# 64 bytes of padding ahead of the two large areas of a transformer kernel's SBUF

## The reference

```
x = x + 0.5 * swiglu(rms_norm(x))                       # ffn1: 1024 -> 2816 -> 1024
x = x + w_out @ (gated gMLP mixer + gated differential attention)   # mixer
x = x + 0.5 * swiglu(rms_norm(x))                       # ffn2
x = x + g1 * w_out_2 @ [S5 state space, sliding-window attention]   # mix2, modulated by c
x = x + g2 * conv_ffn(modulated rms_norm(x))            # ffn3: 1024 -> 2 x 2816, width-3 conv -> 1024
```

## Time and profile before

| what | value |
|---|---|
| time, median of 3 runs | 1828.91 us (1828.8 to 1830.04) |
| the profiled execution's own time | 1823.55 us |
| its span, first to last instruction | 1820.9 us |
| mean granted TensorE clock | 0.994 |
| TensorE busy | 1785.5 us |
| VectorE / ScalarE / GpSimd busy | 1057.2 / 727.5 / 184.5 us |

### The profile page before, as it was taken

One profiled execution on the slowest core, in us unless ns is written; L12 is line 12 of the kernel. 1 busy time (PEld: TensorE's weight loads), 2 busy tenths in 40 slices (PEclk: granted clock), 3 DMA queues, 4 the chain that ended last, 5 costly groups with the idle time before them and its releaser, 6 DMA issues. The chain is left out here.

```text
span 1820.9 us, 23599 instructions
## 1 busy us (share of the span) xinstructions
PE 1785.5 (98%) x8872; PEld 1454.9 (80%) x8872; DVE 1057.2 (58%) x1479; ACT 727.5 (40%) x1011; POOL 184.5 (10%) x239
## 2 busy tenths in 40 slices
PE   8999999999999999999899999999998999999998
PEld 6888888878888777888787888887986778888887
DVE  6666536564564666554789743436585556655433
ACT  3222222333444887423232322224556345555322
POOL 4222001210000000005211020120000400000000
PEclk9999999999999999999899999999999999999999
DMA  7767422333222212223555452335122223222222
GB/s 224 238 216 220 145 72 85 106 117 112 93 77 86 70 48 70 70 93 107 180 165 166 134 168 81 96 101 185 42 100 70 70 93 107 100 92 81 92 89 86
DMA packets 171692, 206.79 MB, mean 114 GB/s; under 512 B 18404, under 2 KB 150114, under 8 KB 171106
## 3 DMA queue, kind: packets, MB, share of 16 engines
q1 hardware_dynamic: 144994, 161.97, 27.5%
q0 software_dynamic: 12640, 38.55, 6.7%
q10 hardware_dynamic: 13984, 5.27, 1.1%
HBM read 190.29 MB, written 17.56 MB: 114 GB/s over the span
## 5 line engine op out<-in xcount | busy, mean ns | idle before, releaser
L662 ACT CAST w_hi<-w_raw 128x2048 fp32r<-128x2048 f32 x158 | 301.3, 1908 | 739.1 <-PE bank L1921 379.9
L1147 DVE TENSOR_TENSOR w_lo<-w_raw,w_hi 128x2048 fp32r<-128x2048 f32 x158 | 367.1, 2324 | 376.3 <-ACT w_hi L662 375.8
L1921 PE MATMUL bank<-h_hi,w_hi 128*128 128x512 f32 x1056 | 414.7, 393 | 6.5 <-DVE w_lo L1147 5.2
L1921 PE MATMUL bank<-h_hi,w_lo 128*128 128x512 f32 x1056 | 412.1, 390 | 0.0
L1921 PE MATMUL bank<-h_lo,w_hi 128*128 128x512 f32 x1056 | 326.3, 390 | 1.6 <-DVE h_lo L1185 1.6
L1921 PEld LDWEIGHTS bank<-h_hi,w_hi 128*128 128x128 f32 x1056 | 199.1, 189 | 51.3 <-issue 5.0
L1921 PEld LDWEIGHTS bank<-h_lo,w_hi 128*128 128x128 f32 x1056 | 198.7, 188 | 43.8 <-DVE h_lo L1185 2.0
L1921 PEld LDWEIGHTS bank<-h_hi,w_lo 128*128 128x128 f32 x1056 | 199.1, 189 | 40.7
L1878 PE MATMUL bank<-hid_hi,w_lo 128*128 128x512 f32 x528 | 205.4, 389 | 0.0
L1878 PE MATMUL bank<-hid_hi,w_hi 128*128 128x512 f32 x528 | 205.4, 389 | 0.0
L1878 PE MATMUL bank<-hid_lo,w_hi 128*128 128x512 f32 x528 | 205.4, 389 | 0.0
(11 more groups left out here) (432 smaller groups left out, 2500.6 us busy)
## 6 DMA issues: line engine op xcount, KB each, us to landing
w_raw<-in_w_in SPq DMA_DIRECT2D x29, 1024.0 KB, 5.0
mod_raw<-in_w_mod POOLq DMA_DIRECT2D x96, 256.0 KB, 3.8
w_raw<-in_ffn_w_gate SPq DMA_DIRECT2D x22, 1024.0 KB, 5.3
w_raw<-in_ffn_w_up SPq DMA_DIRECT2D x22, 1024.0 KB, 5.2
w_raw<-in_w_up SPq DMA_DIRECT2D x22, 1024.0 KB, 4.9
w_raw<-in_ffn_w_down SPq DMA_DIRECT2D x16, 768.0 KB, 4.6
w_raw<-in_ffn_w_down SPq DMA_DIRECT2D x16, 640.0 KB, 3.9
w_raw<-in_w_out SPq DMA_DIRECT2D x8, 1024.0 KB, 5.0
```

The costliest lines, as they stand in the source:

```text
L662: act.copy(w_hi[i % 2][:], w_raw[i % 2][:]).then_inc(S("w_hi_done"), 1)
L1147: dve.tensor_tensor(w_lo[s][:], w_raw[s][:], w_hi[s][:].bitcast(F32), ALU.subtract).then_inc(S("w_split"), 1)
L1921: mm = pe.matmul(bank[:], w[:, k, at], h[:, k, :], start=k == first and part == 0 and i == 0, stop=k == last and part == 1)
```

## The change

A tile without a user is allocated after `rstd` and before `h_area`. It takes 16 floats, 64 bytes, in each partition. All tiles made before it keep their addresses; the two areas and all tiles in them move up by 64 bytes.

```diff
         tmp = sb("tmp", [P, 6, T])
         rstd = sb("rstd", [P, T])
+        sb("past_a_line", [P, 16])
```

## The result

The changed kernel takes 1842.4 us (median of 5 executions, 1841.84 to 1846.85) against 1828.8 (5 executions of the kernel before, 1822.74 to 1830.04): a ratio of 1.009 with an interval of 1.0069 to 1.0111. It is slower by 0.9%, and the forecast was no change. Its profiled execution took 1842.28 us over a span of 1840.7, so the span grew by 19.8 us. The traces of the two kernels are compared with each other.

What follows compares the result with a forecast made beforehand. The prediction took TensorE's matmuls, number times pace, to bound the kernel. Every term was 0, so the sum was 0 and the forecast a median of 1828.9 us, chance 0.63 of nothing to measure; the range was 1825 to 1848 us.

Steps and rivals of the forecast that it cites:

- What bounds the kernel: TensorE, busy 1785.5 of 1820.9 us with few waits: time is the number of matmuls times their pace.
- Matmuls: Matmuls whose moving operand lies in a moved area while the weights don't: 5520, cost taken as 0, bound above 37 us.
- the `ca` rows: Trace of L1993: aligned pairs 0.107 us apart, pairs 64 bytes past a line 0.11 us, read as no difference.
- The lever: One TensorE cycle more, 0.417 ns, in each of 5520 matmuls is 2.3 us; 0.66 ns in each is 3.7 us.
- The count: Matmuls moving an operand from a moved area: gate and up 3168, down 1584, projections 384, L2169 384; 5520 in all.
- Weight loads from moved areas: Token-wise projections loading `h` as weights, some 670: taken as 0, at most 6.7 ns each, 4.5 us.
- a cover of 38 ns: Token-wise projections: a weight load lasts 188 ns of a 226.7 ns pace, so 38 ns cover any slower load.
- VectorE and ScalarE: Operations on moved tiles: both cost 0; VectorE would need 50 ns more in each, ScalarE 0.3 us at most.
- The bound of 3 ns: Sign in the profile after: L1190, L761 and L1183 would stay within 3 ns.
- DMAs: Transfers into or out of moved areas, mainly the input load: taken as 0, at most 7.4 us.
- The first one: Rival: fast matmul stream pays for the offset, 2.3 us a cycle; four cycles 1838 us, sixteen 1866; chance 0.21.
- The third: Rival: offset frees part of the 13 ns above 0.417 ns a column, up to 73 us, 1756 us; chance 0.10.

Runs made afterwards that it cites:

- sweep2: Matmuls alone, whole computation left out, other sizes and types: float32r with 512 columns 226.7, 229.1, 232.4, 233.2 ns at distances 0, 64, 128, 192; float32 429.2 ns a record.
- weights_only: Kernel before with 64 bytes ahead of the weight panels and 448 behind, so only the weight tiles move: 1860.81 us, ratio 1.0193.
- all_64: Kernel before with `up_to_a_line` 64 bytes larger, so x, weight panels, tmp, rstd and both areas move together: 1826.21 us, ratio 1.0002.
- pad_256: The change with 256 bytes of padding instead of 64, against the kernel before: 1828.67 us, ratio 1.0013.
- the sweep: Matmuls alone, computation left out, starts of weights and moving operand varied: with 512 columns 226.7 ns at distance 0, 229.0 at 64, 233.3 at 128 and 192.
- pad_128: The change with 128 bytes of padding instead of 64, against the kernel before: 1859.2 us, ratio 1.018.
- shared_only: Kernel before with the 64 bytes placed after the h area, so only the shared area moves: 1828.11 us, ratio 1.0013.
- h_only: Kernel before with only the h area moved by 64 bytes, the shared area put back on a multiple of 512: 1836.96 us, ratio 1.0055.

## Why the prediction was wrong

**What bounds the kernel:** right. The time is the number of matmuls times their pace, and the change came through the pace.

**Matmuls, "I cost the matmuls at 0 ... by the `ca` rows":** this step failed. The lever was right, 5520 matmuls at 2.3 us a cycle; what each paid was not 0 but 2.2 ns with `hid` moving, and 2.2 to 6.6 ns with `h` moving, in all some 13 us. The `ca` rows could not show it, for three reasons. Those matmuls are plain float32, and sweep2 shows that plain float32 takes the same time at every distance, with 128 columns and with 512 alike. They move 128 columns, with which float32r too has one pace at distances 0 and 64; the caution in the prediction, that a slower stream can hide the cost, pointed at this and was set aside. And `bb` and `ca` both lie in the shared area, where `bb`'s 64-byte pieces advance with `s` as `ca`'s do: moving to `s` = 1 moves both starts by 64 bytes, and `part` adds 128 to `ca`, so that the distances there are 0 and 128 and never 64. The group is indeed unchanged by the change, as both moved together. Before and after:

```profile
L1993 PE MATMUL bank<-ca,bb 64*16 64x128 f32 x128 | 8.4, 270 | 0.0
```

```profile
L1994 PE MATMUL bank<-ca,bb 64*16 64x128 f32 x128 | 8.4, 270 | 0.0
```

The rule that I weighed there, of the Trainium skill, SBUF — State Buffer, section "Door 1: The DMA port swizzle" (a cost for each new line of 16 bytes), gave the same 0; by the runs it doesn't carry over to this offset, since at distance 32, two whole lines, a float32r matmul takes 233.3 ns.

The count was short as well. The products of `ya`, `yb` and `z`, and L1934 and L1939, move an operand of the two areas too, 432 matmuls more. They are in the 13 us with less than 1.

**Weight loads from moved areas, 0:** wrong too, by 4.3 us, against a bound of 4.5 (and 0.9 more in L2075 and L2270, which the count left out). The reason given for the bound (a cover of 38 ns that would be used up) is not what happened: these matmuls stand at distance 192 and take 233 ns for it, and the same happens in weights_only where `w` is loaded. The 96 with 256 columns got faster, by 6.5 ns each (119.9 to 113.4).

**VectorE and ScalarE, 0:** right. The largest group of VectorE on moved tiles, L1191, takes 689 ns where it took 687 in the trace before; L1184 takes 688 for 687, and L762 616 and 618 ns in its two forms for 616 and 617. The bound of 3 ns held.

**DMAs, 0:** right as far as it can be told. TensorE's wait for `x_in` is 1.4 us in all, where it was 0.8. The first matmul of ffn1 started at 18.28 us, not at 17.27; but all_64, whose `x_in` lies at the same offset, starts it at 17.28 with a wait for `x_in` of 1.5 us, and pad_256, whose `x_in` lies on a multiple of 256, waits 0.3. A microsecond of the 19.8 is there and may be one execution's. The rule that the prediction cites from the Trainium skill, DMA: Bandwidth & Descriptors, section "How a descriptor splits into AXI transactions", gives 0.3 us more as an estimate; no run here shows it, as it is too small to be seen in this.

**The rivals.** The first one, with a chance of 0.21, is what happened as to the time, at 5 to 16 cycles where it took four and sixteen as examples. As to the cause it is half right: the fast stream pays, but not for its own offset, since all_64 has the very offset and pays nothing. Of the signs the prediction gave for it the first came (a pace above 227 ns with `h` and `hid` moving) and the second did not: with `w` moving the pace changed the most. That the time lies in the prediction's range, which ends at 1848, is luck: by the same mechanism 128 bytes cost 34 us and 256 bytes nothing. The third had the right observation with the wrong sign: operands that both start on the same multiple do matter, but for 512 columns that is the best place and not the dear one. The 13.3 ns above 0.417 ns a column are not all fixed, though: at 256 columns distance 192 took 6.5 of them away, and at 448 columns 64 took 2.3.

## What to carry to other kernels

Keep the weights and the moving operand of a float32r matmul with 512 columns a multiple of 256 bytes apart within a partition (with 256 or 448 columns another distance was better here): padding one tile and not the other cost 0.9% to 1.9% here, and moving both together cost nothing. Before taking one place of a trace as evidence for another, match the type of the operands and what is held fixed: the evidence used here had another type and moved both operands at once. Read a matmul's cost as the time from start to start (a piece of the chain divided by its count), since the drawn duration went from 389 to 391 ns where the pace went from 226.7 to 228.9.

## What the runs showed of the hardware

- At 2.4 GHz (a mean granted clock of 0.99 and up in every execution), a row of float32r matmuls with 128 x 128 weights and 512 columns takes 226.7 ns each at distance 0, 229 at 64, 232.4 at 128, 233.2 at 192, and 226.7 again at 256. With 256 columns it is 120.0 ns at 0 and 113 to 119 elsewhere in the sweep (120.1 at 128 in pad_128); with 448, 202.5 at 0 and 200.2 at 64. What counts is the distance and not the address: all tiles moved by 64 bytes together cost nothing.
- The same distance can have two paces: 16 (226.7 or 231.7 ns), 240 (226.7 or 233.4), 64 in gate and up of the changed kernel (229 in ffn3, 229 or 233 in ffn1) and with `m` moving (229 there, 233 in shared_only), 192 with 256 columns (113 or 118). A pace once taken lasts: in ffn1 it changed at the small matmuls of L1963 and not between them. In h_only, at the same distance, it is 229.0 ns all through the same stretch. What picks between them is open.
- Plain float32 matmuls take 858 ns with 512 columns, two records of 429.2 ns, whatever the distance.
- No run of float32r matmuls with full weights had a lasting pace under 111.7 ns, from 128 to 240 columns, at distances 0 and 64 alike.
- A shorter weight load (64 or 32 columns of weights) doesn't make the 512-column matmul faster: 230.2 and 231.3 ns at distance 0, against 226.7.
- Executions of one kernel differ by the granted clock: the kernel before has a mean span of 1822.7 us at 0.995 and of 1826.8 at 0.992, so kernels that differ by a few microseconds are compared at the same one.
